# A two-block model on one core: the second block's attention ordered by token tile, its output products between the last groups, and norms kept in PSUM

## The chip, the cores and the metric

The kernel runs on one core of one Trainium2 chip. The time is the device time of one execution in microseconds. One execution was also recorded by the hardware profiler; durations and waits below are from it.

## The reference, cut to what matters

Two blocks of two layers each work on 256 tokens of 1024 features, in float32. The change is in the second block. Each of its layers projects the input, runs three mixers, adds them, normalizes, and runs a feed-forward part:

```
h = x @ w_cols
o_gla  = _gla_mixer(...)      # 4 heads, head norm, times silu(gate)
o_rwkv = _rwkv7_mixer(...)    # 4 heads, head norm, plus bonus, times gate
o_nsa  = _nsa_mixer(...)      # 8 heads: compressed, selected and window attention
mix = jnp.concatenate([o_gla, o_rwkv, o_nsa], axis=-1) @ w_out[l]
x = _layer_norm(DEEPNORM_ALPHA * x + mix, ln1_w[l], ln1_b[l])
ffn = (jax.nn.silu(x @ ffn_w_gate[l]) * (x @ ffn_w_up[l])) @ ffn_w_down[l]
x = _layer_norm(DEEPNORM_ALPHA * x + ffn, ln2_w[l], ln2_b[l])
```

The NSA output is `gt[0] * o_cmp + gt[1] * o_slc + gt[2] * o_win`: the compressed attention (here "block"), the selected one (with 4 blocks of 64 keys and 16 selections it sees every block, so it is causal attention with keys of its own) and the window one.

## The kernel before, in words

Tokens lie in two tiles of 128 partitions. Every engine (PE = TensorE, ACT = ScalarE, DVE = VectorE, POOL = GpSimd, SP = SyncE) runs its own program in the order in which it is written in `second_layers`; semaphores tie them. The same helper names (`nsa`, `gla`, ...) stand in the program of each engine.

Weights are multiplied in two parts of reduced precision. An item is 256 rows by up to 512 columns. SP loads it into one of three raw slots, ACT casts it (`W.high`, L172) into one of four parts slots, POOL subtracts the cast from the raw item (`W.low`, L179), and PE multiplies (`W.multiply`, L210): per item and token tile 2 chunks x 3 products = 6 matmuls of 512 columns. ACT's cast of item k waits until PE has used item k - 4 for both tiles; POOL takes the items in order.

The attention of the selected (kind 0) and window (kind 1) branch comes in 12 groups `GROUPS2`: kind, token tile, key-value group and, in tile 1, a half. `nsa(a)` on PE issues the scores of group a (bank 4), the turn of group a-1's probabilities (bank 5) and the values of group a-2 (bank 0); DVE (`soft`, `output`) reads scores, takes the maximum and scales the sums into `NS`; ACT does the exponentials and copies turned probabilities. Between groups stand the steps of the two recurrent mixers (`gla`, `increment`, `unknowns`, `from_state`, `outputs`). Probabilities live in `sm` and `PT`, which lie in the fourth parts slot, and the block attention's tiles in the third; so no weight of `w_out` is split before the attention is over.

After group 11 come, in this order: the block attention's values (`block_values`, L1471; scores and turn stand before groups 12 and 13 of the pipeline), the turns of `NS` over both tiles, four NSA items of `w_out` (`out_nsa(n)`: columns half n // 2, rows half n % 2, both tiles), the turns of the normed mixer outputs `Y`, and four items for these (`out_mix`), tile after tile. `centre`, `spread` and `scale` on DVE are the head norm; ACT applies its weights into `VAL` (L2022), DVE `mixed` multiplies by gates and splits high and low. `residual` adds `ALPHA * x` in `x` and takes statistics; `layer_norm` normalizes `x` in SBUF in two steps of 1024 columns (L2097). Then `x` is turned and the first gate columns are multiplied tile by tile. The down products use banks 0 and 1.

## Time and profile before

| | us |
| --- | --- |
| median of 3 runs | 1605.82 (1604.97 to 1606.61) |
| the profiled execution | 1605.48 |
| its span | 1603.7 |
| PE busy | 1513.7 |
| POOL busy | 973.1 |
| ACT busy | 788.6 |
| DVE busy | 724.8 |

The span runs from the first to the last recorded instruction. A busy PE is not PE at its peak: matmuls overlap, and the clock granted to it has two levels, 1.2 and 2.4 GHz; the profile gives its mean over a stretch as a share of full speed. An engine's idle time costs something only where another waits for it.

### The profile page before, as it was taken

The page shows a single profiled execution, that of the slowest core. Times are in us where ns is not written, and L with a number is a line of the kernel's source. Part 1 is how long each engine was busy: PE and PEld are TensorE (multiplying, and loading weights), DVE is VectorE, ACT ScalarE, POOL GpSimd, SP SyncE. Part 2 cuts the span into 40 slices and gives each one's busy share as a digit, 9 for nine tenths or more (in the row PEclk, how much of TensorE's full clock was granted, in tenths as well). Part 3 has the DMA queues.
Part 4 walks back from the last instruction along what each step waited for, and adds up shares of the span by engine and source line. Part 5 has one row for each costly group of instructions (what it writes and reads, how often), then busy time and mean ns, then how long its engine had stood idle before and what let it go on. Part 6 is the DMA issues. An engine that isn't in the chain of part 4 may idle for free. (4 is left out here: it accounts for less than half of the span.)

```text
span 1603.7 us, 20620 instructions
## 1 busy us (share of the span) xinstructions
PE 1513.7 (94%) x7896; PEld 1243.0 (78%) x7896; DVE 724.8 (45%) x1078; ACT 788.6 (49%) x1230; POOL 973.1 (61%) x416
## 2 busy tenths in 40 slices
PE   8999999999999998989999889999899998799998
PEld 6887787778886886768788668888688786678886
DVE  3224835562218562625567671110346667721102
ACT  5544575445445664358454434443476443444442
POOL 6887349787884386767200269879774000778785
PEclk9999999999999999999999799999999998899999
DMA  7665335455663255555311136655453310456553
GB/s 228 182 177 165 92 93 179 159 174 166 183 183 106 81 156 182 173 167 148 118 48 54 53 118 201 207 157 205 144 169 96 106 53 1 132 160 188 150 197 131
DMA packets 121632, 227.96 MB, mean 142 GB/s; under 512 B 10304, under 2 KB 26176, under 8 KB 121536
## 3 DMA queue, kind: packets, MB, share of 16 engines
q1 hardware_dynamic: 120384, 222.46, 45.5%
q10 hardware_dynamic: 1152, 4.19, 0.9%
q8 instruction: 63, 1.03, 0.3%
q14 instruction: 33, 0.27, 0.1%
HBM read 225.58 MB, written 1.05 MB: 141 GB/s over the span
## 5 line engine op out<-in xcount | busy, mean ns | idle before, releaser
L179 POOL TENSOR_TENSOR parts<-raw,parts 128x1024 fp32r<-128x1024 f32 (+5 forms) x412 | 972.9, 2376 | 616.4 <-ACT parts L172 614.0
L210 PE MATMUL ps<-parts,xT 128*128 128x512 f32 (+4 forms) x2624 | 819.9, 390 | 20.1 <-issue 4.4
L172 ACT CAST parts<-raw 128x1024 fp32r<-128x1024 f32 (+5 forms) x412 | 415.6, 1013 | 458.6 <-PE ps L210 251.0
L210 PEld LDWEIGHTS ps<-parts,xT 128*128 128x128 f32 x2624 | 493.5, 191 | 128.6 <-issue 10.6
L210 PE MATMUL ps<-parts,x_low 128*128 128x512 f32 (+3 forms) x672 | 254.7, 387 | 0.0
L210 PE MATMUL ps<-parts,M_low 128*128 128x512 f32 (+2 forms) x640 | 245.3, 387 | 0.0
L210 PEld LDWEIGHTS ps<-parts,x_low 128*128 128x128 f32 x672 | 129.1, 192 | 23.7 <-issue 0.5
L210 PEld LDWEIGHTS ps<-parts,M_low 128*128 128x128 f32 x640 | 121.3, 190 | 20.6
L210 PE MATMUL ps<-parts,aT 128*128 128x512 f32 x352 | 109.5, 395 | 0.0
L210 PE MATMUL ps<-parts,H_low 128*128 128x512 f32 x272 | 106.0, 394 | 0.0
L210 PEld LDWEIGHTS ps<-parts,aT 128*128 128x128 f32 x352 | 66.0, 187 | 15.6
L2585 DVE TENSOR_TENSOR EE<-ps,EE 128x512 f32<-128x512 f32 (+1 forms) x24 | 15.3, 646 | 103.5 <-ACT EE L2065 103.3
L706 ACT ACTIVATE H<-ps,st 128x512 f32<-128x512 f32 (+2 forms) x72 | 47.3, 666 | 28.5 <-PE ps L210 28.1
L210 PE MATMUL ps<-parts,ysT 128*128 128x512 f32 x192 | 61.1, 396 | 0.0
L210 PEld LDWEIGHTS ps<-parts,H_low 128*128 128x128 f32 x272 | 51.0, 188 | 12.3
L2592 DVE TENSOR_TENSOR H<-ps,EE 128x512 f32<-128x512 f32 (+1 forms) x24 | 15.5, 647 | 96.4 <-PE ps L210 96.4
L2536 DVE SCALAR_TENSOR_TENSOR x<-x,ps 128x512 f32<-128x512 f32 x16 | 10.9, 679 | 103.7 <-PE ps L210 103.7
L767 ACT ACTIVATE sm<-sm,nmx 128x256 f32<-128x256 f32 (+1 forms) x80 | 36.3, 457 | 29.5 <-DVE nmx L944 29.5
L210 PE MATMUL ps<-parts,mn_high 128*128 128x512 f32 x128 | 44.4, 415 | 0.4 <-DVE mn_low L821 0.4
L1252 PE MATMUL ps<-ident,H 128*128 128x128 f32 x228 | 34.5, 286 | 9.1 <-DVE H L2086 8.0
L1252 PEld LDWEIGHTS ps<-ident,H 128*128 128x128 f32 x228 | 28.6, 147 | 18.2 <-DVE H L2086 12.2
L210 PEld LDWEIGHTS ps<-parts,ysT 128*128 128x128 f32 x192 | 36.1, 188 | 8.5
(340 smaller groups left out, 1825.1 us busy)
## 6 DMA issues: line engine op xcount, KB each, us to landing
raw<-in_w_in SPq DMA_DIRECT2D x160, 512.0 KB, 3.5
raw<-in_ffn_w_down SPq DMA_DIRECT2D x44, 512.0 KB, 4.4
raw<-in_ffn_w_gate SPq DMA_DIRECT2D x40, 512.0 KB, 3.7
raw<-in_ffn_w_up SPq DMA_DIRECT2D x40, 512.0 KB, 3.7
raw<-in_w_out SPq DMA_DIRECT2D x32, 512.0 KB, 3.4
raw<-in_w_branch SPq DMA_DIRECT2D x24, 512.0 KB, 3.3
raw<-in_w_mem_kv SPq DMA_DIRECT2D x16, 512.0 KB, 3.4
raw<-in_w_in SPq DMA_DIRECT2D x16, 366.0 KB, 3.2
```

The source lines that it names most:

```text
L172: self.nc.scalar.copy(self.part(i, 0)[:, 0:nk, 0:w], self.raw(i)[:, 0:nk, 0:w]).then_inc(self.hi_ready.sem, 1)
L179: self.nc.gpsimd.tensor_tensor(self.part(i, 1)[:, 0:nk, 0:w], self.raw(i)[:, 0:nk, 0:w], self.part(i, 0)[:, 0:nk, 0:w], ALU.subtract).then ...
L210: ins = pe.matmul(b[:, 0:w], a(k0 + 2 * n + c, t), self.part(i, lo_w)[:, c, 0:w], start=(opens and n == p == 0), stop=(final and p == len( ...
L706: PJ.empty(lane, nc.scalar.activation(H[:, t, c0:c0 + w], b[:, 0:w], ACT.Sigmoid if s in TAIL_STEPS else ACT.Copy, scale=st[:, 0, t:t + 1] ...
L767: lane.done(nc.scalar.activation(smv(a, j), smv(a, j), ACT.Exp, bias=nmx[:, a, j:j + 1], accum_out=den[:, a, j:j + 1]), p_ok if j == 3 els ...
L1252: ins = pe.transpose(b[:, k * P:(k + 1) * P], src, chip.ident[:])
L2536: banks.empty(lane, v.scalar_tensor_tensor(out=xs, in0=xs, scalar=ALPHA, in1=b[:, :], op0=ALU.mult, op1=ALU.add), ((s, j), t), L)
L2585: PJ.empty(lane, v.tensor_tensor(sg[:, t, 0:w], b[:, 0:w], sg[:, t, 0:w], ALU.mult), (("gt", j), t))
L2592: ins = v.tensor_tensor(H[:, t, c0:c0 + w], b[:, 0:w], sg[:, t, 0:w], ALU.mult)
```

## The change

Seven edits, all in the second block. `GROUPS2` and `SUMS2` run over tiles first, so that all of tile 0's attention is done with group 3. The block attention moves up: its scores before group 6, its turn before 7, its values (into bank 1) before 8 and 9; DVE's and ACT's parts of it move with it. From group 6 on, probabilities go to `KPt` and `BAt`, two tiles of the recurrence that are free by then, and `tmp` to `IC`; so ACT casts the four NSA items between groups 7 and 10, and POOL makes their low parts there. `NS` is turned by tile, and `out_nsa` and `out_mix` take one tile at a time, the first of them before and after the last values. The head norm, the weighting and the mix work in the PSUM banks that the products wrote, ACT takes the squares; `residual` and `layer_norm` work in PSUM in halves of 512 columns and write `x` once, and PE turns each half when it is written. The output columns close half by half: the first half for both tiles, then the second tile by tile. The down products get banks 4 to 7 (`DB`). Of the gate columns' items ACT casts two ahead of the root and two behind the turned `x`, where it cast one and three.

```diff
-GROUPS2 = [(k, t, g, q) for k in range(2) for t in range(NT) for g in range(2) for q in range(t + 1)]
-SUMS2 = [(k, t, g) for k in range(2) for t in range(NT) for g in range(2)]
+GROUPS2 = [(k, t, g, q) for t in range(NT) for k in range(2) for g in range(2) for q in range(t + 1)]
+SUMS2 = [(k, t, g) for t in range(NT) for k in range(2) for g in range(2)]
 G2 = len(GROUPS2)
+BLOCK_AT = 6
+MOVED = 6
...
+    def turn_n(t):
+        pe.wait_ge(*E("ns").at((1, 1 + len(SUMS2) // 4)[t]))
+        turn(("n", t), [NS[:, t, c * P:(c + 1) * P] for c in range(4)])
+    def out_nsa(n, tiles):
+        for t in tiles:
+            TP.taken(pe, ("n", t))
+            if (n, t) == (0, 0):
+                BO.drained(pe, ("block", 1))
+            if (n, t) == (2, 0):
+                pe.wait_ge(*E("o_read").at(len(SUMS2)))
+            W.multiply(pe, ("out_nsa", n // 2), n % 2, by_feature(OT), by_feature(x_lo), [t])
+    def turn_y(t):
+        YB.taken(pe, ("Y", t))
+        turn(("y", t), [Y[:, t, c * P:(c + 1) * P] for c in range(4)])
+    def out_mix(j, n, t):
+        TP.taken(pe, ("y", t))
+        W.multiply(pe, ("out_mix", j), n, by_feature(OT), by_feature(x_lo), [t])
...
     increment(2)
+    block_scores()
     nsa(6)
     from_state(2)
     unknowns(3)
     gla(4)
     from_state(3)
+    block_turn_p()
     nsa(7)
     gla(5)
+    block_values(0)
     nsa(8)
     gla(6)
+    block_values(1)
     nsa(9)
     for par in range(2):
         GB.taken(pe, (("g", LEVELS), par))
     outputs(0)
+    turn_n(0)
     nsa(10)
+    nsa(11)
     outputs(1)
-    nsa(11)
-    block_scores()
     nsa(12)
-    block_turn_p()
+    out_nsa(0, [0])
     nsa(13)
+    out_nsa(1, [0])
+    turn_n(1)
+    out_nsa(2, [0])
+    out_nsa(0, [1])
+    out_nsa(1, [1])
+    turn_y(0)
+    out_nsa(2, [1])
+    out_nsa(3, [0])
+    turn_y(1)
+    out_nsa(3, [1])
+    for n in range(2):
+        for t in range(NT):
+            out_mix(0, n, t)
     for t in range(NT):
-        block_values(t)
-    pe.wait_ge(*E("ns").at(NT))
-    turn(("n", 0), [NS[:, t, c * P:(c + 1) * P] for c in range(2) for t in range(NT)])
-    turn(("n", 1), [NS[:, t, c * P:(c + 1) * P] for c in range(2, 4) for t in range(NT)])
-    for n in range(4):
-        out_nsa(n)
-        if n % 2:
-            t = n // 2
-            pe.wait_ge(*E("normed").at(t + 1))
-            turn(("y", t), [Y[:, t, c * P:(c + 1) * P] for c in range(4)])
-    ST.drained(pe, ("Y", 1))
+        for n in range(2):
+            out_mix(1, n, t)
     for t in range(NT):
-        pe.wait_ge(*E("mixed").at(t + 1))
-        for j in range(2):
-            for n in range(2):
-                W.multiply(pe, ("out_mix", j), n, by_feature(OT), by_feature(x_lo), [t])
-    for t in range(NT):
-        pe.wait_ge(*E("x1").at(t + 1))
         for i in range(2):
+            OB.taken(pe, (("out", i), t))
...
     nsa(6)
+    act.wait_ge(*E("mxc").at(1))
+    lane.done(sc.activation(spare[2][:, 0:256], spare[2][:, 0:256], ACT.Exp), E("pc_exp"))
     between(2)
     decayed(5)
     between(3)
-    for a in range(7, G2 + 1):
-        nsa(a)
-    act.wait_ge(*E("mxc").at(1))
-    lane.done(sc.activation(spare[2][:, 0:256], spare[2][:, 0:256], ACT.Exp), E("pc_exp"))
-    act.wait_ge(*E("pt_full").at(G2 + 1))
-    lane.done(sc.copy(spare[2][:, 256:512], ptb[:, 0:S]), E("pt"))
-    for t in range(NT):
+    act.wait_ge(*E("bpt_full").at(1))
+    lane.done(sc.copy(spare[2][:, 256:512], ptb[:, 0:S]), E("bpt"))
+    def squares(t):
+        act.wait_ge(*E("centred").at(t + 1))
+        lane.done(sc.activation(CUM[:, 2 * t:2 * t + 2, :].rearrange("p m n -> p (m n)"), YB.read(act, ("Y", t)),
+                                ACT.Square), E("squared"))
+    def n_high(t):
+        b = TP.read(act, ("n", t))
+        lane.done(sc.copy(OT[:, 4:8, t * P:(t + 1) * P], b.rearrange("p (c n) -> p c n", c=4)), E("n_high"))
+    def deviation(t):
         act.wait_ge(*E("var").at(t + 1))
         eight = slice(8 * t, 8 * t + 8)
         lane.done(sc.activation(st[:, 2, eight], st[:, 1, eight], ACT.Sqrt), E("sd"))
-    act.wait_ge(*E("o_read").at(len(SUMS2) + NT))
-    W.high(act, W.begin(("out_nsa", 0)) + 1)
-    for i in range(2):
-        b = TP.read(act, ("n", i))
-        lane.done(sc.copy(OT[:, 4 + 2 * i:6 + 2 * i, :], turned(b)), E("n_high"))
-    W.high(act, W.begin(("out_nsa", 0)) + SPLIT - 1)
+    first = W.begin(("out_nsa", 0))
+    nsa(7)
+    W.high(act, first)
+    nsa(8)
+    W.high(act, first + 1)
+    nsa(9)
+    BO.wait_filled(act, ("block", 1))
+    W.high(act, first + 2)
+    n_high(0)
+    nsa(10)
+    W.high(act, first + 3)
+    nsa(11)
+    squares(0)
+    nsa(12)
+    deviation(0)
+    n_high(1)
+    squares(1)
+    deviation(1)
+    W.high(act, first + SPLIT)
+    W.high(act, first + SPLIT + 1)
...
         if k == 0:
-            W.high(act, first_gate)
+            W.high(act, first_gate + 1)
         root(0)
         if k == 0:
+            x1_high(0)
             W.high(act, first_gate + 3)
-            x1_high(0)
         if k == 0 or l == layers - 1:
...
-        b = ST.read(dve, ("Y", t))
+        b = YB.read(dve, ("Y", t))
         TP.taken(dve, ("I", 2 * t + 1))
-        lane.settle()
-        ST.empty(lane, v.tensor_tensor(Y[:, t, :], b[:, :], Y[:, t, :], ALU.add), ("Y", t))
+        tt(b[:, :], b[:, :], Y[:, t, :], ALU.add)
         yv, _, mean, _, _ = norm(t)
         lane.settle()
         lane.done(v.tensor_reduce(mean, yv, AX_X, ALU.add))
         ts(mean, mean, 1.0 / HD, None, ALU.mult)
-        tt(yv, yv, mean.unsqueeze(2).to_broadcast([P, 8, HD]), ALU.subtract)
+        tt(yv, yv, mean.unsqueeze(2).to_broadcast([P, 8, HD]), ALU.subtract, E("centred"))
     def spread(t):
         yv, sv, inv, var, sd = norm(t)
-        tt(sv, yv, yv, ALU.mult)
-        lane.settle()
+        dve.wait_ge(*E("squared").at(t + 1))
...
     def mixed(t):
         n = slice(t * P, (t + 1) * P)
-        TP.taken(dve, ("y", t))
-        tt(VAL[:, 0:2, n], VAL[:, 0:2, n], FT[:, F_GG:F_GG + 2, n], ALU.mult)
-        tt(VAL[:, 2:4, n], VAL[:, 2:4, n], BON[:, :, n], ALU.add, settle=False)
-        tt(VAL[:, 2:4, n], VAL[:, 2:4, n], GT[:, :, n], ALU.mult)
+        b = TP.read(dve, ("y", t)).rearrange("p (c n) -> p c n", c=4)
+        dve.wait_ge(*E("weighted").at(t + 1))
+        tt(b[:, 0:2], b[:, 0:2], FT[:, F_GG:F_GG + 2, n], ALU.mult)
+        tt(b[:, 2:4], b[:, 2:4], BON[:, :, n], ALU.add, settle=False)
+        tt(b[:, 2:4], b[:, 2:4], GT[:, :, n], ALU.mult)
         lane.settle()
-        lane.done(v.tensor_copy(OT[:, 0:4, n], VAL[:, :, n]))
-        tt(x_lo[:, 0:4, n], VAL[:, :, n], OT[:, 0:4, n], ALU.subtract, E("mixed"))
+        lane.done(v.tensor_copy(OT[:, 0:4, n], b))
+        lane.settle()
+        TP.empty(lane, v.tensor_tensor(x_lo[:, 0:4, n], b, OT[:, 0:4, n], ALU.subtract), ("y", t))
+    def n_low(t):
+        b = TP.read(dve, ("n", t))
+        dve.wait_ge(*E("n_high").at(t + 1))
+        n = (slice(None), slice(4, 8), slice(t * P, (t + 1) * P))
+        TP.empty(lane, v.tensor_tensor(x_lo[n], b.rearrange("p (c n) -> p c n", c=4), OT[n], ALU.subtract), ("n", t))
...
     grown(2)
+    block_soft()
     nsa(6)
     step(3)
     gla(4)
+    block_sums()
     nsa(7)
     gla(5)
+    block_output(0)
     nsa(8)
     gla(6)
     nsa(9)
+    block_output(1)
+    nsa(10)
+    n_low(0)
+    nsa(11)
     centre(0)
-    nsa(10)
+    nsa(12)
     spread(0)
-    nsa(11)
-    block_soft()
+    nsa(13)
+    n_low(1)
     centre(1)
-    nsa(12)
+    scale(0)
     spread(1)
-    nsa(13)
-    block_sums()
-    block_output(0)
-    block_output(1)
-    for i in range(2):
-        low(x_lo[:, 4 + 2 * i:6 + 2 * i, :], ("n", i), OT[:, 4 + 2 * i:6 + 2 * i, :], i, "n_high")
-    scale(0)
     scale(1)
     mixed(0)
     mixed(1)
...
     def residual(banks, s, j, t, L=L):
         b = banks.read(dve, ((s, j), t), L)
-        xs = x[:, t, j * HALF:(j + 1) * HALF]
-        banks.empty(lane, v.scalar_tensor_tensor(out=xs, in0=xs, scalar=ALPHA, in1=b[:, :],
-                                                 op0=ALU.mult, op1=ALU.add), ((s, j), t), L)
         lane.settle()
-        lane.done(v.bn_stats(bn[:, t, j, :], xs))
-    def layer_norm(k, t, l=l):
+        lane.done(v.scalar_tensor_tensor(out=b, in0=x[:, t, j * HALF:(j + 1) * HALF], scalar=ALPHA, in1=b,
+                                         op0=ALU.mult, op1=ALU.add))
+        lane.settle()
+        lane.done(v.bn_stats(bn[:, t, j, :], b))
+    def layer_norm(k, t, l=l, L=L):
+        banks, s = ((OB, "out"), (DB, "dn"))[k]
         lane.settle()
         lane.done(v.bn_aggr(mv[:, t, :], bn[:, t, :, :].rearrange("p a b -> p (a b)")))
         ts(mv[:, t, 1:2], mv[:, t, 1:2], LN_EPS, None, ALU.add, e=E("lnv"))
         dve.wait_ge(E("ln_in").sem, 64 * (l + 1))
-        stt(x[:, t, :], x[:, t, :], mv[:, t, 0:1], ln[:, 2 * k, :], ALU.subtract, ALU.mult, settle=False)
+        for j in range(2):
+            b = banks.read(dve, ((s, j), t), L)
+            stt(b, b, mv[:, t, 0:1], ln[:, 2 * k, j * HALF:(j + 1) * HALF], ALU.subtract, ALU.mult, settle=False)
         dve.wait_ge(E("lns").sem, 2 * NT * l + NT * k + t + 1)
         lane.done(v.reciprocal(mv[:, t, 1:2], mv[:, t, 1:2]))
-        stt(x[:, t, :], x[:, t, :], mv[:, t, 1:2], ln[:, 2 * k + 1, :], ALU.mult, ALU.add, E("x2" if k else "x1"))
+        lane.settle()
+        for j in range(2):
+            b, half_ = banks.read(dve, ((s, j), t), L), slice(j * HALF, (j + 1) * HALF)
+            banks.empty(lane, v.scalar_tensor_tensor(out=x[:, t, half_], in0=b, scalar=mv[:, t, 1:2], in1=ln[:, 2 * k + 1, half_],
+                                                  op0=ALU.mult, op1=ALU.add), ((s, j), t), L)
...
+        DB = Banks(ctx, nc, "db", [chip.bank(4 + i) for i in range(4)])
```

What this does to PE's order at the end of the attention, in the first layer (L1430 before and L1444 after are turns of probabilities, L1446 and L1460 values, L1471 block values, L1252 and L1262 turns, L210 products with weights). Before:

```order
L1430 MATMUL ps<-ident,spare_3_7037 128x128 [waits e_pt,e_p]
L1430 MATMUL ps<-ident,spare_3_7037 128x128 x3
L1446 MATMUL ps<-H,spare_3_7037 128x64 [waits e_o_read,e_pt]
L1446 MATMUL ps<-H,spare_3_7037 128x64 x3
L1463 MATMUL ps<-ident,spare_2_7036 128x128 [waits e_pt,e_pc_exp]
L1463 MATMUL ps<-ident,spare_2_7036 128x128
L1446 MATMUL ps<-H,spare_3_7037 128x64 [waits e_pt]
L1446 MATMUL ps<-H,spare_3_7037 128x64 x3
L1471 MATMUL ps<-spare_2_7036 128x512 [waits tp_emptied1,e_pt,e_o_read]
L1471 MATMUL ps<-spare_2_7036 128x512 [waits e_o_read]
L1252 MATMUL ps<-ident,H 128x128 [waits tp_emptied1,e_ns]
L1252 MATMUL ps<-ident,H 128x128 x3
```

After:

```order
L1444 MATMUL ps<-ident,H 128x128 [waits e_pt,e_p]
L1444 MATMUL ps<-ident,H 128x128 x3
L1460 MATMUL ps<-H 128x64 [waits e_o_read,e_pt]
L1460 MATMUL ps<-H 128x64 x3
L210 MATMUL ps<-parts,xT 128x512 [waits w_high_ready,bo_emptied0,tp_emptied1]
L210 MATMUL ps<-parts,x_low 128x512
L210 MATMUL ps<-parts,xT 128x512
L210 MATMUL ps<-parts,x_low 128x512
L210 MATMUL ps<-parts,xT 128x512 [waits w_low_ready]
L210 MATMUL ps<-parts,xT 128x512
L1460 MATMUL ps<-H 128x64 [waits e_pt]
L1460 MATMUL ps<-H 128x64 x3
```

The block values are gone from here, and one tile's product with the first item stands between the values of groups 10 and 11; the wait for `e_ns` has gone to the turn behind it.

ACT's order in the first layer, before from the copy of group 10's turned probabilities on, after from group 9's exponentials on (L1916 and L1950 are such copies, L1909 and L1943 exponentials, L172 casts of weights, L2017 and L2049 high parts of `NS`, L2044 squares, L2012 and L2054 roots). Before:

```order
L1916 COPY spare_3_7037<-ps 128x512 [waits e_o_full,e_pt_full]
L1909 ACTIVATE spare_3_7037,den<-spare_3_7037,nmx 128x256 [waits e_mx]
L1909 ACTIVATE spare_3_7037,den<-spare_3_7037,nmx 128x256
L1916 COPY spare_3_7037<-ps 128x512 [waits e_o_full,e_pt_full]
L2006 ACTIVATE spare_2_7036<-spare_2_7036 128x256 [waits e_mxc]
L2008 COPY spare_2_7036<-ps 128x256 [waits e_pt_full]
L2012 ACT_TABLE_LOAD
L2012 ACTIVATE st<-st 128x8 [waits e_var] x2
L172 CAST parts<-raw 128x1024 [waits w_landed2,w_used,e_o_read]
L172 CAST parts<-raw 128x1024 [waits w_landed0,w_used]
```

After:

```order
L1943 ACTIVATE H,den<-H,nmx 128x256 [waits e_mx]
L1943 ACTIVATE H,den<-H,nmx 128x256
L172 CAST parts<-raw 128x1024 [waits w_landed1,w_used,bo_filled]
L2049 CAST xT<-ps 128x4x128 [waits tp_filled]
L1950 COPY H<-ps 128x512 [waits e_o_full,e_pt_full]
L1943 ACTIVATE H,den<-H,nmx 128x256 [waits e_mx]
L1943 ACTIVATE H,den<-H,nmx 128x256
L172 CAST parts<-raw 128x1024 [waits w_landed2,pj_filled]
L1950 COPY H<-ps 128x512 [waits e_o_full,e_pt_full]
L1943 ACTIVATE H,den<-H,nmx 128x256 [waits e_mx]
L1943 ACTIVATE H,den<-H,nmx 128x256
L2044 ACTIVATE CUM<-ps 128x512 [waits yb_filled,e_centred]
```

Casts, which stood behind everything, stand between the exponentials and the next copy, and the squares ahead of the last copy.

## Rows read from the trace of the kernel before

**Rows 1.** The page: span, and busy time of each engine.

```profile
span 1603.7 us, 20620 instructions
...
PE 1513.7 (94%) x7896; PEld 1243.0 (78%) x7896; DVE 724.8 (45%) x1078; ACT 788.6 (49%) x1230; POOL 973.1 (61%) x416
...
L179 POOL TENSOR_TENSOR parts<-raw,parts 128x1024 fp32r<-128x1024 f32 (+5 forms) x412 | 972.9, 2376 | 616.4 <-ACT parts L172 614.0
```

**Rows 2.** Windows: PE, PEld, DVE, ACT, POOL busy us, granted clock, DMA share, GB/s.

```profile
863.30:959.90 96.60, 80.69 (x446) 65.11 (x447) 71.75 (x117) 41.25 (x85) 34.96 (x14) 0.88 0.21 66
1319.80:1330.30 10.50, 10.50 (x77) 9.87 (x75) 6.60 (x13) 4.61 (x13) 0.00 (x0) 0.84 0.01 2
1330.30:1353.50 23.20, 22.15 (x183) 20.03 (x182) 20.02 (x45) 10.08 (x32) 0.00 (x0) 1.00 0.00 1
1353.50:1366.65 13.15, 6.18 (x14) 2.57 (x13) 8.79 (x22) 5.28 (x8) 3.06 (x2) 0.56 0.00 0
1366.65:1381.40 14.75, 14.74 (x56) 11.63 (x56) 9.05 (x9) 5.48 (x9) 10.67 (x5) 0.82 0.42 143
1381.40:1395.95 14.55, 11.76 (x48) 8.79 (x48) 14.07 (x13) 5.81 (x9) 9.74 (x5) 1.00 0.48 144
1395.95:1401.90 5.95, 2.13 (x10) 1.76 (x10) 5.23 (x6) 1.64 (x2) 5.95 (x2) 0.78 0.63 175
1401.90:1409.45 7.55, 7.55 (x25) 5.91 (x26) 5.45 (x9) 0.79 (x2) 2.53 (x2) 0.72 0.49 140
1409.45:1416.40 6.95, 6.71 (x34) 5.43 (x33) 1.98 (x3) 5.89 (x7) 2.36 (x2) 1.00 0.01 2
1319.80:1416.40 96.60, 81.72 (x440) 65.97 (x439) 71.18 (x115) 39.57 (x80) 34.31 (x14) 0.86 0.22 66
```

**Rows 3.** Waits of PE, 1319.8 to 1416.4: us, times, longest.

```profile
PE ps L1471 <- DVE spare L2086: 4.0, 2, 3.2
PE ps L1252 <- DVE x L2097: 3.8, 1, 3.8
PE ps L210 <- issue: 2.2, 1, 2.2
```

**Rows 4.** Timeline of DVE: start, us, instruction, idle before it.

```profile
1137.43 3.32 DVE L2097 SCALAR_TENSOR_TENSOR x<-x,mv,arena 128x1024 f32<-128x1024 f32 x1
...
1369.15 2.45 DVE L2086 TENSOR_TENSOR H<-H,st 128x512 f32<-128x512 f32 x1
...
1378.21 2.52 DVE L2469 CAST xT<-DL 128x512 fp32r<-128x512 f32 x1
...
1388.60 0.43 DVE L2086 TENSOR_TENSOR DL<-DL,GT 128x256 f32<-128x256 f32 x1
...
1393.35 3.25 DVE L2097 SCALAR_TENSOR_TENSOR x<-x,mv,arena 128x1024 f32<-128x1024 f32 x1
...
1399.79 0.67 DVE L2536 SCALAR_TENSOR_TENSOR x<-x,ps 128x512 f32<-128x512 f32 x1
```

**Rows 5.** Timeline of POOL: four low parts.

```profile
1393.10 11.33 POOL L179 TENSOR_TENSOR parts<-raw,parts 128x1024 fp32r<-128x1024 f32 x4 [4.81 <-ACT parts L172]
```

**Rows 6.** Timeline of ACT: two casts of weights, and the norm's weighting.

```profile
1362.46 1.99 ACT L172 CAST parts<-raw 128x1024 fp32r<-128x1024 f32 x2 [6.24 <-DVE spare L2086]
...
1375.41 1.51 ACT L2022 ACTIVATE DL<-ps,vec2s 128x128 f32<-128x128 f32 x4 [4.83 <-PE ps L1252]
```

**Rows 7.** Timeline of PE: a wait at the layer change, one at 1319, block products.

```profile
1140.80 1.09 PE L1252 MATMUL ps<-ident,x 128*128 128x128 f32 x8 [2.53 <-DVE x L2097]
...
1319.12 0.71 PE L1574 MATMUL ps<-H 64*128 64x128 f32 x4 [1.30 <-DVE H L2483]
...
1348.35 1.92 PE L1455 MATMUL ps<-spare,arena 128*128 128x32 f32 x16
...
1356.78 2.07 PE L1471 MATMUL ps<-spare 128*128 128x512 f32 x2 [3.21 <-DVE spare L2086]
```

**Rows 8.** The chain that ended last: start, us, what.

```profile
1463.55 22.18 PE ps L210 x96
```

122 lines of the change are left out of this document (67 added, 55 removed).

## The prediction

> **What bounds the kernel now.** I read the page first: TensorE (PE) is busy for 1513.7 of 1603.7 us [rows 1], so only some 90 us of idle time, and time at the lower clock, can be won. Then the windows: in the first of the second block's two layers, 863.3 to 959.9, PE is busy for 80.69 us of 96.60, in the second, 1319.8 to 1416.4, for 81.72 [rows 2]. The two are one picture 456.5 us apart, so I work out one and count it twice. The stretch runs from the third state increment to the end of the first gate columns; the change touches no other place but the layer change and the very end.
>
> The windows by stage show where that stretch loses. From 1353.5 to 1366.65 PE works 6.18 us of 13.15 at a mean granted clock of 0.56: block values, sums and turns of the attention output, one after another. From 1381.4 to 1401.9 it idles twice more (2.79 and 3.82 us) [rows 2]. Its waits say for whom: DVE's block sums (4.0), the layer norm's `x` (3.8), the mix (2.2, shown as issue) [rows 3]. Why DVE is late stands in its timeline: with POOL at work a 128x512 product of two SBUF operands took 2.45, a cast 2.52, a 128x1024 step of the layer norm 3.25, while `x<-x,ps`, with one operand in PSUM, took 0.67 in the same stretch of POOL work, 1393.10 to 1404.43 [rows 4, 5].
>
> Ledger of the 96.6 us: idle 96.60 - 81.72 = 14.9. A clock of 0.84, 0.56, 0.82, 0.78 and 0.72 means that a share of twice the missing part was granted 1.2 instead of 2.4 GHz (32, 88, 36, 44, 56%); half of the busy time in that share is lost: 1.7 + 2.7 + 2.7 + 0.5 + 2.1 = 9.7. Left is work at full clock: 81.7 - 9.7 = 72.0.
>
> **The change, part by part.** No product of PE is added or removed, so the 72.0 stay. What changes are the waits and the clock. I walk PE's new order from 1319.8 with the durations of before. One tile of one output piece is 6 matmuls of 22.18/96 = 0.231 us [rows 8], so 1.4.
>
> *Groups by token tile.* The first tile's four sums are done before the stretch; one of them adds a multiply and an add on DVE ahead of a step PE waits for: +0.4.
>
> *Block attention moved up.* `block_scores` (1.92 [rows 7]) stands before group 6, and group 6's scores now wait for DVE to read its bank: idle 0.6, before these two reads came behind the scores at no cost. Two block values (2.07 each at the low clock [rows 7], 1.06 at the upper) go between groups, where their inputs are long ready: the 4.0 and the wait for the turns behind them go. Late next is DVE, 20.02 of 23.2 us busy there [rows 2]; the moved sums and outputs (some 4.5 us of DVE) stand against one sum taken out ahead of it and 6 us of PE work put between the groups.
>
> *Weights split during the attention.* Four casts of 1.0 [rows 6] enter ACT between groups 7 and 10, behind the exponentials, ahead of the copy of the next group's turned probabilities, which PE needs later: nothing. But each releases a POOL instruction of 2.4 [rows 1], and the attention has DVE steps with two SBUF operands. Bounds for a lock: 0 and 2.5 (the 128x512 product [rows 4]). Walked through, `block_output(0)`, the sum of groups 4-5, `block_output(1)` and `output(6)` wait 0.7, 1.9, 0.8 and 0.8; PE has other work behind most of it: idle 0.5 before the turn of group 10. The 1.9 falls on a 128x4 product, a size that no row shows under POOL.
>
> The Trainium skill (SBUF — State Buffer, "Who interferes with whom") says that a DVE instruction with two SBUF inputs and a GpSimd one that reads SBUF exclude each other for the whole instruction, whoever issues first. The trace agrees at 2.45 against 0.67. It speaks against this part, and for the PSUM part; taken for every size it gives the walk above, and with small steps exempt some 2 us less a layer.
>
> *Output products between the last groups.* `values(11)` stands behind ACT's `squares(0)`, and that behind `centre(0)` on DVE, 4 steps of up to 0.7: idle 1.1. Then turn, high part and low part of tile 1 hide behind the 1.4 of the pieces around them; `turn_y(0)` waits 0.3 for `scale(0)`.
>
> *Norm and mix.* All eight NSA pieces end near 1370.7, against 1381.4 before. The mix is late next: DVE's `spread(1)`, the root, then on ACT two casts (2.0), only then the weighting (1.51) [rows 6], then `mixed(0)` on DVE in PSUM, 3 x 0.43 + 2 x 0.7 = 2.9 with gaps, against 2.52 + 2.7 for its last two steps before: ready at 1373.3, idle 2.6. `mixed(1)` ends 2.9 later and one piece (1.4) lies between: idle 1.5.
>
> *Output columns half by half.* The last two pieces of tile 0 end 2.8 before the last product. The norm then takes 1.5 (sum, statistics), 0.5 (aggregate), 1.3 (first pair, halves of 0.67), 0.1, 0.75 (first half of the last pair): idle 4.2 - 2.8 = 1.4 for the first turn, instead of 3.82. POOL can't hold it, since all steps read PSUM. Then 0.8 until the first product (0.5 for the high part, 0.3 at the second tile).
>
> *Casts of the gate columns.* Only two of the four are ahead of the root now; two stand behind `x1_high(0)`. Their low parts need 1.0 + 2.4 and another 2.4: PE waits 1.3 and 1.0 in the first tile.
>
> Idle after: 0.4 + 0.6 + 0.5 + 1.1 + 0.3 + 2.6 + 1.5 + 1.4 + 0.8 + 1.3 + 1.0 = 11.5. Before, the clock fell after idle of 3.8 us, after 7.0 in pieces, and also around one wait of 1.30 at 1319 [rows 2, 7]. I keep the 1.7 of the first window and one drop as priced at 1401.9 (2.1) [rows 2]: 3.8; bounds 0 and 9.7. Layer: 72.0 + 11.5 + 3.8 = 87.3 against 96.6, gain 9.3, twice 18.6.
>
> *Layer change.* PE waits 2.53 for `x` there [rows 7], whose last step took 3.32 under POOL [rows 4]. As two halves in PSUM of 0.67 it ends 2.0 sooner, and the first turn needs only the first of them. I take 2.2 for both tiles; bounds 1.3 (something else is as late) and 3.2 (all 2.5, and a half step at the second tile). *The end*: four steps of 512 take what two of 1024 did; 0.
>
> Sum: 18.6 + 2.2 = 20.8 off the profiled execution's 1605.48 (its span of 1603.7 and 1.8 around it), 0.3 under the median of 1605.82: 1584.7, I say 1585.
>
> **Rivals.**
> *A. The clock holds and small steps pass POOL.* PE's gaps become many and short instead of few and long, and 23.2 us with 1.05 idle ran at 1.00 [rows 2]. Without the 3.8 and the 2 of locks per layer: 1584.7 - 11.6 = 1573. Against it: the drop around 1.30 us of idle at 1319 [rows 7].
> *B. Each of the four locks falls on the path in full.* DVE is 86% busy in the attention, and sets PE's scores. 4 x 2.5 = 10 on PE's path, of which the walk's 0.5, 1.1 and some of the mix's wait hold about 3: +7 a layer, 1599. Against it: the PE work now lying between the groups.
> *C. POOL bounds the gate columns.* The first tile consumes a piece in 1.4, POOL makes one in 2.4 to 2.8 [rows 1, 5]. If all four came late: 4 x 2.6 - 5.6 = 4.8 instead of 2.3, 1590. Against it: two are split during the mix.
> *D. Slower: the lower clock takes the attention.* If the locks thin PE's work between groups so far that 1.2 GHz is granted there, matmul time doubles, and each us of full-clock work costs another. It decides from 10.4 us of such work a layer beyond what the forecast holds (20.8/2); with 14 the time is 1584.7 + 28 = 1613. Before, a stretch of 11.6 us at the low clock went with 7.0 us of idle [rows 2], and the attention's 23.2 us with 1.05 of idle had none.
> *E. It doesn't overlap:* a wait in ACT's order (the split behind the block values) holds the turned copies back, and PE's tail only moves. Then the loss of 1353.5 to 1381.4 (7.0 idle, 5.4 clock) stays instead of 3.9 (0.5, 1.1, 0.3 and half of the clock's 3.8): a layer gains 9.3 - 8.5 = 0.8, in all 3.8, 1602.
>
> **Chances.** Forecast 0.50, A 0.19, B 0.14, C 0.08, D 0.05, E 0.04. About 3.2 us (0.2%) is what a measurement tells from no change. Faster 0.92, same 0.03, slower 0.05. Likeliest case's own range 1578 to 1592; eight times in ten 1571 to 1599.
>
> **What would show it.** The window from 1353.5 on has no stretch at 0.56, and PE's idle over the same work is 10 to 12 us, not 14.9. DVE steps with two SBUF operands between groups 7 and 11 take up to 2.5 where POOL works, the norm's halves 0.67 always. PE waits for `mixed(0)` 2 to 3 us, for the norm's first half 1 to 2, for POOL in the gate columns about 2. I am wrong if PE waits over 3 us anywhere in the attention (B or D), if the clock there is under 0.9, or if the mix is ready before the NSA pieces end (A and more).

## The result, and the profile after

The changed kernel takes 1599.35 us (median of 20 runs, 1592.0 to 1620.29) where the kernel before takes 1608.15 in the same rounds: a ratio of 0.995, 95% interval 0.9935 to 0.9966, so 8 to 9 us faster. Run once more, unaltered, on another chip it was 1592.05 beside 1605.73, ratio 0.9909 (0.9891 to 0.9928): 14 us. The forecast was 1585, 20.8 us off. The direction was right; the size was too large by 12 to 13 us on the first chip and by 7 on the second.

The two kernels differ in how much one execution differs from the next. The kernel before keeps within 1600 and 1615 on all chips; the changed one goes from 1587 to 1620, and its time follows its mean granted clock: 1592.0 at 0.983, 1599 near 0.979, 1608.3 at 0.970, 1620.3 at 0.962, 1.1 us for each 0.001 in a line through the 20. All ratios here leave out executions more than 1.5% above the fastest of their kernel, which the medians keep; the profile that came with the result is of such an execution (1620.3), so the readings below are from the repeat (1594.34 us, clock 0.981).

The page of that execution, its span and the first section, against [rows 1]:

```profile
span 1593.0 us, 20692 instructions
...
PE 1518.0 (95%) x7896; PEld 1247.3 (78%) x7896; DVE 701.7 (44%) x1090; ACT 788.7 (50%) x1234; POOL 964.8 (61%) x416
```

DVE's work is 23 us less than before; TensorE's is 4 us more, although no product was added. Where that comes from stands in four windows (busy time of each engine, then the granted clock): from the first state increment to the end of the third, and from there to the turn of x1's second tile, in both layers. First of before, then of after.

```profile
852.95:864.75 11.80, 10.15 (x86) 9.05 (x87) 7.43 (x17) 6.32 (x19) 0.00 (x0) 1.00 0.60 178
864.75:952.25 87.50, 72.58 (x407) 58.42 (x406) 69.21 (x112) 33.57 (x73) 31.96 (x12) 0.86 0.23 73
1308.00:1319.85 11.85, 10.19 (x86) 9.10 (x87) 7.43 (x17) 6.21 (x19) 0.00 (x0) 1.00 0.63 178
1319.85:1409.40 89.55, 74.91 (x406) 60.45 (x406) 69.20 (x112) 33.68 (x73) 31.95 (x12) 0.85 0.23 71
```

```profile
852.05:867.90 15.85, 15.10 (x85) 13.84 (x85) 9.58 (x22) 6.32 (x19) 0.00 (x0) 0.68 0.45 133
867.90:948.25 80.35, 70.14 (x398) 55.71 (x399) 57.24 (x109) 32.65 (x67) 28.43 (x12) 0.96 0.24 73
1301.35:1318.20 16.85, 16.61 (x84) 14.86 (x84) 9.10 (x21) 6.06 (x19) 0.00 (x0) 0.59 0.45 126
1318.20:1398.65 80.45, 70.30 (x399) 55.80 (x399) 57.12 (x109) 32.64 (x67) 28.41 (x12) 0.96 0.24 73
```

The forecast's stretch is, but for gate columns at its end, the second and the fourth row: 87.50 to 80.35 and 89.55 to 80.45, 16.3 us gained where 18.6 were forecast. The second layer gained 9.1 of the 9.3 forecast, the first only 7.2: it was 2 us shorter before, so working out one layer and counting it twice took too much. The lower clock there went from 0.86 and 0.85 to 0.96. But the rows above them, the state chain, went from 11.80 to 15.85 and from 11.85 to 16.85: the same products at a granted clock of 0.68 and 0.59 instead of 1.00. TensorE's busy time there rose by 4.95 and 6.42, its idle time fell by 0.90 and 1.42. Of those 9.1 us the forecast has only its 0.4 a layer for the added sum. With 2.7 at the layer change, 0.9 gained ahead of the first increment and nothing at the end, that is 16.3 + 2.7 + 0.9 - 9.1 = 10.8, but for rounding the difference of the spans (1603.7 - 1593.0 = 10.7). Over the whole span TensorE's idle time fell by 15.0 us (90.0 to 75.0) where the forecast had 9.0, and its busy time rose by 4.3 where the forecast had it fall by 11.8.

What TensorE waited for in the forecast's stretch, in place of [rows 3] (us in total, times, longest):

```profile
PE ps L210 <- DVE x_low L2530: 3.1, 2, 2.0
PE ps L210 <- POOL parts L179: 1.8, 2, 1.1
PE ps L1262 <- DVE x L2622: 1.5, 1, 1.5
PE ps L1460 <- ACT H L1950: 1.1, 1, 1.1
PE ps L1444 <- ACT H L1943: 0.7, 1, 0.7
PE ps L1430 <- DVE spare L2154: 0.6, 1, 0.6
PE ps L1262 <- DVE H L2516: 0.6, 1, 0.6
PE ps L1430 <- DVE H L2154: 0.6, 1, 0.6
```

With two of 0.2 that are left out, together 10.4; the forecast had 11.1 here, and 0.4 ahead of it. The waits of 4.0, 3.8 and 2.2 us are gone.

### The profile page after: what moved, and what is told of

Read it like the earlier page. It is cut to its first block and busy times, and to the rows that moved or that the text cites. A ratio compares the mean times of both kernels' runs of the same rounds, so it can differ in the third digit from the quotient of the medians.

```text
span 1619.0 us, 20692 instructions
## 1 busy us (share of the span) xinstructions
PE 1544.4 (95%) x7896; PEld 1268.1 (78%) x7896; DVE 705.7 (44%) x1090; ACT 787.7 (49%) x1234; POOL 965.2 (60%) x416
## 5 line engine op out<-in xcount | busy, mean ns | idle before, releaser
L210 PE MATMUL ps<-parts,xT 128*128 128x512 f32 (+4 forms) x2624 | 818.2, 389 | 21.9 <-DVE x_low L2530 5.7
L172 ACT CAST parts<-raw 128x1024 fp32r<-128x1024 f32 (+5 forms) x412 | 415.5, 1012 | 439.5 <-PE ps L210 240.5
L210 PEld LDWEIGHTS ps<-parts,xT 128*128 128x128 f32 x2624 | 491.1, 190 | 130.3 <-ACT parts L172 10.8
L210 PE MATMUL ps<-parts,x_low 128*128 128x512 f32 (+3 forms) x672 | 253.9, 386 | 0.0
L210 PE MATMUL ps<-parts,M_low 128*128 128x512 f32 (+2 forms) x640 | 244.5, 386 | 0.0
L210 PEld LDWEIGHTS ps<-parts,x_low 128*128 128x128 f32 x672 | 128.5, 191 | 23.0 <-issue 0.5
L210 PEld LDWEIGHTS ps<-parts,M_low 128*128 128x128 f32 x640 | 120.7, 189 | 20.4
L210 PE MATMUL ps<-parts,aT 128*128 128x512 f32 x352 | 110.1, 395 | 1.2 <-POOL parts L179 1.2
L210 PE MATMUL ps<-parts,H_low 128*128 128x512 f32 x272 | 106.0, 394 | 0.0
L210 PEld LDWEIGHTS ps<-parts,aT 128*128 128x128 f32 x352 | 66.0, 188 | 17.6 <-POOL parts L179 2.1
L2602 DVE SCALAR_TENSOR_TENSOR ps<-x,ps 128x512 f32<-128x512 f32 x16 | 11.1, 696 | 116.8 <-PE ps L210 115.8
L210 PE MATMUL ps<-parts,ysT 128*128 128x512 f32 x192 | 61.1, 396 | 0.0
L210 PEld LDWEIGHTS ps<-parts,H_low 128*128 128x128 f32 x272 | 51.0, 188 | 12.2
L210 PE MATMUL ps<-parts,mn_high 128*128 128x512 f32 x128 | 44.0, 412 | 0.9 <-DVE mn_low L821 0.4
L210 PEld LDWEIGHTS ps<-parts,ysT 128*128 128x128 f32 x192 | 36.1, 188 | 8.5
L1262 PE MATMUL ps<-ident,H 128*128 128x128 f32 x228 | 33.8, 280 | 7.3 <-DVE H L2143 4.9
L1262 PEld LDWEIGHTS ps<-ident,H 128*128 128x128 f32 x228 | 27.5, 144 | 14.7 <-DVE H L2143 6.8
```

The source lines that it names most:

```text
L172: self.nc.scalar.copy(self.part(i, 0)[:, 0:nk, 0:w], self.raw(i)[:, 0:nk, 0:w]).then_inc(self.hi_ready.sem, 1)
L210: ins = pe.matmul(b[:, 0:w], a(k0 + 2 * n + c, t), self.part(i, lo_w)[:, c, 0:w], start=(opens and n == p == 0), stop=(final and p == len( ...
L1262: ins = pe.transpose(b[:, k * P:(k + 1) * P], src, chip.ident[:])
L2602: lane.done(v.scalar_tensor_tensor(out=b, in0=x[:, t, j * HALF:(j + 1) * HALF], scalar=ALPHA, in1=b, op0=ALU.mult, op1=ALU.add))
```

## The experiments

Each time stands beside the kernel before on the same chip in the same rounds. The kernels before of different rows ran on different chips, so rows are compared by their ratios. In the table "clock" is the range of the mean granted clock over a kernel's executions. Each name says what the kernel starts from, "before" or "changed".

| kernel | us, median | before | ratio, 95% interval | clock |
|---|---|---|---|---|
| changed, again | 1592.05 | 1605.73 | 0.9909 (0.9891 to 0.9928) | 0.981-0.987 |
| before + group order | 1609.22 | 1605.73 | 1.0023 (1.0012 to 1.0034) | 0.969-0.973 |
| before + group order, sum late | 1605.55 | 1605.95 | 1.0003 (0.9988 to 1.0018) | 0.970-0.981 |
| before + 16 products of 32 columns | 1614.30 | 1606.23 | 1.0052 (1.0035 to 1.0069) | 0.971-0.973 |
| before + norm in PSUM | 1604.47 | 1605.73 | 0.9990 (0.9980 to 1.0001) | 0.972-0.981 |
| the same + order of gate casts | 1598.09 | 1605.60 | 0.9950 (0.9936 to 0.9964) | 0.975-0.981 |
| changed + transposes in chain | 1597.37 | 1605.73 | 0.9940 (0.9920 to 0.9960) | 0.976-0.989 |
| changed, sum late | 1594.11 | 1605.95 | 0.9931 (0.9907 to 0.9956) | 0.978-0.987 |
| changed, sums mixed | 1598.67 | 1605.95 | 0.9940 (0.9915 to 0.9965) | 0.961-0.985 |
| the same, casts late | 1595.14 | 1605.95 | 0.9931 (0.9917 to 0.9946) | 0.980-0.985 |
| changed, sum late, states early | 1621.52 | 1605.60 | 1.0079 (1.0055 to 1.0103) | 0.945-0.981 |
| the same, squares late | 1632.97 | 1605.60 | 1.0168 (1.0116 to 1.0219) | 0.945-0.962 |
| the same, fifth level moved | 1622.78 | 1605.60 | 1.0084 (1.0052 to 1.0116) | 0.959-0.975 |
| changed, sum late, dense fill in chain | 1590.75 | 1606.23 | 0.9902 (0.9880 to 0.9924) | 0.984-0.995 |
| changed, sum late, transposes in chain | 1599.65 | 1606.23 | 0.9948 (0.9925 to 0.9971) | 0.977-0.989 |
| the dense fill, attention too | 1586.30 | 1606.23 | 0.9882 (0.9860 to 0.9904) | 0.986-0.994 |
| the same, mix and norm too | 1587.40 | 1605.12 | 0.9879 (0.9854 to 0.9903) | 0.990-0.995 |
| before + dense fill | 1595.22 | 1605.12 | 0.9938 (0.9918 to 0.9959) | 0.989-0.994 |

### 1. The changed kernel again

No edit. 

> The changed kernel once more, unaltered. Theory of the clock: the walk of waits was about right (in the first layer of the profiled execution 84.6 us stand where 96.6 stood), and the 14 us that the median of 1599 lacks to 1585 are time at 1.2 GHz, which starts at the two waits of 0.8 and 0.7 us in the state chain (850 and 852 us) and in some executions lasts through the attention. Then the times spread over more than 10 us with the mean granted clock, by some 1.3 us for each 0.001 of it, and the drop near 852 and 1302 is there again, of another length. Rival, a fixed cost (locks, the new order of the groups): the times keep within 5 us of their median and the clock explains no more than 2 us.

The low clock near 856 and 1303 us was there again; the spread on this chip was small (five executions, 1586.9 to 1594.3; a sixth, of 2969.64 us at a clock of 1.0, is unexplained and left out of the ratio; without it the median is 1590.98). This is how the low clock begins. TensorE around the first increment, then DVE in the same time (start, duration, instruction, in brackets the idle time before it and its releaser):

```profile
852.06 1.13 PE L1599 MATMUL ps<-H 64*128 64x128 f32 x8 [0.76 <-ACT LD L2012]
853.92 0.37 PE L1605 MATMUL ps<-H 64*128 64x128 f32 x1 [0.73 <-DVE H L2545]
```

```profile
849.90 0.17 DVE L2314 RECIPROCAL fac<-den 128x4 f32<-128x4 f32 x1
850.53 0.17 DVE L2143 TENSOR_TENSOR fac<-fac,gate 128x4 f32<-128x4 f32 x1 [0.46 <-DVE fac L2314]
850.73 0.42 DVE L2143 TENSOR_TENSOR IC<-ps,fac 128x256 f32<-128x256 f32 x1
851.19 0.42 DVE L2143 TENSOR_TENSOR H<-H,IC 128x256 f32<-128x256 f32 x1
...
853.59 0.28 DVE L2545 COPY H<-EE 64x256 f32<-64x256 f32 x1
```

Four steps of the third group's sum, `fac` to `H<-H,IC`, 1.7 us with their wait, stand ahead of the state step `H<-EE` at 853.59, for which the increment waits 0.73. There is the forecast's "one of them adds a multiply and an add on DVE ahead of a step PE waits for: +0.4", at 1.8 times its price in this layer and about half of it (0.23) in the other. What follows it is larger, in windows of 5 us (the granted clock is the first of the last three numbers):

```profile
850.00:855.00 5.00, 3.50 (x27) 3.09 (x26) 3.36 (x9) 2.34 (x7) 0.00 (x0) 1.00 0.52 154
855.00:860.00 5.00, 5.00 (x25) 4.44 (x24) 3.51 (x9) 2.85 (x9) 0.00 (x0) 0.58 0.92 265
860.00:865.00 5.00, 5.00 (x30) 4.78 (x30) 2.76 (x7) 0.46 (x1) 0.00 (x0) 0.50 0.01 4
```

### 2. The group order, and one sum

```diff
-GROUPS2 = [(k, t, g, q) for k in range(2) for t in range(NT) for g ...
-SUMS2 = [(k, t, g) for k in range(2) for t in range(NT) for g ...
+GROUPS2 = [(k, t, g, q) for t in range(NT) for k in range(2) for g ...
+SUMS2 = [(k, t, g) for t in range(NT) for k in range(2) for g ...
```

On the kernel before, alone: 

> The kernel before with the groups ordered by token tile, nothing else. Theory that the order brings the drop in the state chain: the clock falls at about 1300 to 1310 us and near 855, and stays low for 10 us or more, time 2 to 8 us over the kernel before. Theory that the order is innocent: the 0.4 us a layer of the forecast, between 0 and +1.5 us in all, and the clock in 840 to 870 us at 0.95 or more.

3.5 us slower, with low stretches behind the first increment in both layers. In the profiled execution the three increments take 5 to 6 us more in each layer; in the second, the kernel before has a low stretch behind the third increment (0.83 from 1320 to 1330), which this one lacks (0.58 there while the chain still runs, then 1.00), so part of it comes back. Then the same with the sum behind the step:

```diff
-                nsa(4)
+                nsa(4, summed=False)
...
                 grown(0)
+                output(2)
                 nsa(5)
```

> The kernel before with the groups ordered by token tile and the third group's sum moved behind the first state step. The order alone gave 1609.2 beside 1605.7. Theory of the sum: back to the kernel before, within 1.5 us of it, and no low stretch of 13.7 us at 854 and 1315. Rival: still 3 us above it.

Back to the kernel before (1.0003). The windows 850 to 870, order alone and then with the sum late, and of the latter one window in the second layer:

```profile
850.00:860.00 10.00, 8.51 (x44) 7.32 (x42) 5.58 (x15) 4.41 (x15) 0.00 (x0) 0.69 0.73 210
860.00:870.00 10.00, 10.00 (x59) 9.07 (x59) 5.85 (x14) 3.10 (x9) 0.00 (x0) 0.62 0.01 3
```

```profile
850.00:860.00 10.00, 8.77 (x69) 7.89 (x69) 7.77 (x17) 4.11 (x11) 0.00 (x0) 1.00 0.52 129
860.00:870.00 10.00, 7.83 (x70) 6.84 (x69) 7.38 (x18) 5.29 (x15) 0.00 (x0) 1.00 0.23 84
...
1310.00:1320.00 10.00, 8.90 (x49) 7.75 (x50) 6.15 (x16) 4.57 (x15) 0.00 (x0) 0.69 0.70 211
```

So in the kernel before one sum ahead of the state step costs some 3 us (the two intervals overlap by a little, 1.0012 to 1.0018), and by the windows of the first layer it is clock. The second layer says that the sum isn't the only way in: in this execution (1610.51 us, one of the slower of its twelve) the increment waits for no sum, and the clock still falls at 1314, behind one wait of 0.87 us, for 10 us. In the changed kernel moving the sum should have brought 6 to 12 us:

> The changed kernel with one sum of the groups moved on DVE: the one of the third group runs behind the first state step instead of ahead of it. Theory that the sum opens the door to the low clock: ahead of the step it costs 1.9 us of DVE, the first increment waits 0.7 us (0.3 in the second layer) behind a wait of 0.8, and the clock falls for 10 to 14 us. With the sum behind the step the second wait goes, the clock stays up in 840 to 870 us and 1300 to 1320, first to third increment take 8.7 to 10 us instead of 14 to 15, and the time is 1580 to 1586 where the changed kernel had 1592. Rival, the clock falls there in any case because of what the groups of the first tile hold: time within 3 us of the changed kernel.

It did not (0.9931, not to be told from 0.9909). The first low stretch went, and TensorE then waited 1.08 us twice, in the second and third increment; the clock fell behind the second of these, where the changed kernel has its block scores:

```profile
863.11 0.71 PE L1605 MATMUL ps<-H 64*128 64x128 f32 x4 [1.08 <-DVE H L2549]
863.75 1.97 PE L1469 MATMUL ps<-spare,arena 128*128 128x32 f32 x16
866.30 2.07 PE L1430 MATMUL ps<-arena 64*128 64x256 f32 x4 [0.58 <-DVE spare L2154]
```

The last of these rows takes 2.07 us, where the same products take 1.13 at full clock.

Nor did another order of the sums help, which keeps the fifth group free of one (`SUMS2 = [(0,0,0), (0,0,1), (0,1,0), (1,0,0), (1,0,1), (0,1,1), (1,1,0), (1,1,1)]`):

> The changed kernel with another order of the sums: the first group of the second tile before the second kind of the first, so that no sum falls into the group ahead of the first state step (as in the kernel before). Theory of the sum: as for the kernel with the sum moved, 1578 to 1586. The first tile's sums are ready one group later, which turn_n(0) may wait for: up to 0.5 us a layer. Rival as there: 1590 or more, with a low stretch of over 10 us behind the first increment.

1598.67, from 1589 to 1622; a low stretch behind the third increment in both layers of the profile.

### 3. The block scores' place

```diff
                 increment(2)
+                pe.wait_ge(*E("sc_read").at(6))
+                pe.wait_ge(*E("kblk").at(1))
+                for t in range(NT):
+                    for c in range(4):
+                        pe.matmul(scb[...], qT[:, c, t * P:(t + 1) * P], kblk, start=True, stop=True)
                 nsa(6)
```

> The kernel before with the 16 products of 32 columns that the changed kernel has behind the third increment, here without a reader (1.1 us of TensorE at full clock). If this light work behind the third wait is what lets the clock fall there, a low stretch of 7 us or more between 861 and 880 and 4 to 10 us slower than the kernel before. If it is only work: 0 to 2.2 us slower and the clock up there.

8.1 us slower. The 8 calls are recorded as 16 products, and they are not the 1.1 us that was expected: [rows 7] has them at 1.92 us, in a window at full clock [rows 2]. So 3.5 to 3.8 of the 8.1 us are their own time in two layers, and some 4.4 come on top. The kernel before and then this one, 860 to 870:

```profile
860.00:870.00 10.00, 8.70 (x74) 8.01 (x72) 6.92 (x15) 5.19 (x16) 0.00 (x0) 1.00 0.06 23
```

```profile
860.00:870.00 10.00, 8.70 (x44) 8.10 (x44) 4.26 (x8) 2.85 (x7) 0.00 (x0) 0.65 0.01 2
```

In this layer the clock stays up behind a wait of 1.3 us in the one and falls behind the same wait in the other. In the second layer it falls in both, for 3 to 4 us in the kernel before (0.83 from 1320 to 1330) and for some 10 in this one. In the repeat of the changed kernel the clock had fallen before the block scores began; with the sum moved they stand where it falls. So they are a second way in, and would explain why undoing the first did not help. The changed kernel with its block scores moved back was not run.

### 4. Filling the waits

First with transposes of the identity, before the first increment (6), in each increment (3) and before group 6 (4):

> The changed kernel with 6, 3 a step and 4 transposes without a reader put into TensorE's waits of the state chain (before the first increment, before the unknowns of each increment, before group 6). Theory of the clock: with the waits filled the low stretches at 850 and 1302 us go, the attention runs at 2.4 GHz in nearly every execution, mean clock 0.985 or more, median 1580 to 1592, spread half of the changed kernel's. Rival, the fill is only work on the path: some 19 transposes of 0.13 us a layer, half of them hidden, 2 to 3 us slower than the changed kernel, with the same clock.

No gain on the changed kernel (0.9940 against 0.9909): the chain's second and third increment still waited (1.5 us), and the low stretch came 8 and 11 us later. Then with work that is there anyway: on top of the late sum, `from_state(1)` and `from_state(2)` each moved ahead of the increment that waits:

```diff
                 unknowns(1)
+                from_state(1)
                 increment(1)
                 gla(3)
-                from_state(1)
                 unknowns(2)
+                from_state(2)
                 increment(2)
                 block_scores()
                 nsa(6)
-                from_state(2)
```

> The changed kernel with the third group's sum behind the first state step, and the products from the state of the second and third chunk ahead of the increments instead of behind them: 1.3 us of work that was there anyway now lies in the two waits of 1.1 us in the state chain. Theory of the clock (a wait there, with little else around it, opens a low stretch of 7 to 14 us, and filling it with work that is there anyway closes it): no low stretch in 840 to 885 and 1290 to 1335 us, 2.2 us of idle a layer gone too, time 1582 to 1589. Rival, the low stretch only moves to the next wait, as it did with the transposes and with the sum moved: within 3 us of those kernels, 1591 to 1597.

1621.52, 16 us slower than the kernel before, where 1582 to 1589 was expected, the largest miss of the study. The waits of 1.08 went; in their place stands one of 2.34, for ACT's copy out of the bank that the moved product fills. Its row, and then the clock behind it:

```profile
862.95 1.22 PE L1614 MATMUL ps<-SP,DL 128*128 128x128 f32 x4 [2.34 <-ACT H L2027]
```

```profile
870.00:890.00 20.00, 19.42 (x83) 16.71 (x84) 10.48 (x25) 6.44 (x16) 1.19 (x1) 0.50 0.00 0
890.00:910.00 20.00, 20.00 (x71) 14.75 (x70) 11.25 (x17) 5.02 (x12) 5.33 (x3) 0.50 0.15 53
910.00:930.00 20.00, 20.00 (x84) 17.88 (x84) 8.80 (x17) 6.82 (x15) 2.87 (x2) 0.50 0.15 53
930.00:940.00 10.00, 9.36 (x42) 6.91 (x42) 5.08 (x12) 1.71 (x4) 0.00 (x0) 0.94 0.00 0
```

From 890 on TensorE is busy for 20.00 of 20 us, and it is granted 1.2 GHz through the whole attention; the full clock comes back at 931, where the NSA output columns of 512 begin. That is what rival D described, though no lock set it off. The wait of 2.34 stands right ahead of it; no run takes that wait alone out, so that it is the cause is not shown. Two edits on top of it, ACT's `squares(0)` behind `nsa(12)`, and the fifth level's products ahead of group 6, were meant to take out the next waits:

> The kernel with the states early, and in it ACT's squares of the first tile behind the last group's copy instead of ahead of it. The wait of 1.1 us of values(11), which the forecast named, goes: 2.2 us off in two layers if nothing else is as late, and the low stretch that begins at 899 or 1347 us in some executions begins less often: 2 to 8 us faster than the states early. Rival: the copy then waits for something else on TensorE or DVE, within 1 us.

> The same, and the fifth level's products between the block scores and group 6, where TensorE waits 0.6 us for the block's softmax to read the bank. Another 1.2 us in two layers, 0 to 3 us faster than the squares late, by the theory of the clock; nothing, if DVE sets the pace of the chain.

1632.97 and 1622.78, where 2 to 8 us less than the states early, and up to 3 less again, were expected: no gain shows at this clock. Most executions of the states early and the squares late come in groups, near 1621 and near 1645; their profiles, one from each group, show the attention at 1.2 GHz in one layer, and in both.

Then both kinds of work at the same places, the sum late in both: before the first increment 3, in the second and third 4, before group 6 2 products (5, 7 and 4 transposes).

```diff
+                def filler(n, copies):
+                    pe.wait_ge(*E("pt").at(copies))
+                    for _ in range(n):
+                        pe.matmul(ptb[:, :], xT[:, 0, 0:P], xT[:, 0:2, :].rearrange("p c s -> p (c s)"), start=True, stop=True)
```

> The changed kernel with the third group's sum behind the first state step, and products of 128x512 without a reader put into the waits of the state chain: 3 before the first increment, 4 in each of the next two, 2 between block scores and group 6 (0.23 us each). Theory that light work around a wait starts the low stretch and dense work keeps the clock: no low stretch in 840 to 885 and 1290 to 1335, 1582 to 1590. Rival, the wait alone counts and these fills hide in it: the same result for the transposes. Rival, the low stretch comes a few us later all the same: 1592 to 1598.

> The same with transposes of 128x128 in place of the dense products, as long in all (5, 7 and 4 for 3, 4 and 2). If the kind of work counts, low stretches of 7 to 14 us behind the chain as in the kernels before, some of them long, 1592 to 1605. If only the waits count, as fast as the dense fill.

0.9902 against 0.9948, on one chip; the intervals just miss each other. Against its own base, the late sum alone (0.9931), the dense fill in the chain is not clear of noise. The profiled execution with dense products has no low stretch from the chain to the gate columns, in either layer; the other keeps the clock in the chain and loses it in the attention (dense first):

```profile
850.00:870.00 20.00, 19.50 (x146) 16.24 (x145) 13.35 (x32) 8.01 (x24) 0.00 (x0) 1.00 0.27 103
...
890.00:910.00 20.00, 17.01 (x106) 13.75 (x106) 15.13 (x29) 7.78 (x17) 2.36 (x1) 1.00 0.16 54
910.00:930.00 20.00, 16.30 (x71) 12.31 (x69) 12.25 (x25) 9.17 (x16) 14.27 (x6) 1.00 0.52 148
```

```profile
850.00:870.00 20.00, 18.84 (x150) 16.43 (x148) 14.23 (x34) 8.18 (x22) 0.00 (x0) 1.00 0.33 107
...
890.00:910.00 20.00, 18.72 (x105) 17.00 (x105) 13.37 (x21) 8.84 (x20) 5.71 (x3) 0.74 0.25 80
910.00:930.00 20.00, 16.25 (x67) 11.89 (x66) 11.74 (x25) 8.13 (x16) 9.43 (x4) 0.89 0.28 80
```

So in the chain both fills held the clock, in the first layer of these two executions. They are no fair pair: the dense one is the fastest of its six (1583.21), the other the slowest of its seven (1602.02). That the dense kind is better rests on the ratios, not on a place. Filling the attention's waits as well (2 and 3 around group 11's scores, 4 before the last values), and then those of mix and norm (6, 4, 5):

> d_chain, and dense products in the attention's three waits as well: 2 before group 11, 3 between its scores and the turn, 4 before the last group's values, 2.1 us in waits of 2.3. By the theory of the clock the low stretches of 1347 and 899 us go too, mean clock 0.985 or more in every execution, 1578 to 1586, spread under 6 us. Rival, the fills come on top: 2 to 4 us slower than d_chain.

> d_all, and dense products in the waits of the tail: 6 and 4 before the first mix products (waits of 1.9 and 1.2 us), 5 before the turn of x1 (1.5 us). If low stretches still begin there in some executions, 1 to 4 us faster than d_all's 1586, mean clock 0.993 or more. If not, the same time within 1.5 us.

1586.30 and 1587.40, ratios 0.9882 and 0.9879: the fastest versions here, for 22 and 37 products a layer that nobody reads. The first is clear of the changed kernel's result (0.995), and of the late sum alone (0.9931, on the same chip); from the repeat's 0.9909 it can't be told. The tail's fill adds nothing. Nor do the fills always hold the clock: in the profiled execution of the first (1593.87, the slowest of its six) it fell at 1317 in the second layer, behind the block scores, with dense products in each wait of the chain (0.90 and 0.76 in the two windows from 1310 to 1330), and again from 1370 on. The control is the kernel before with fills in its own waits, 45 a layer:

> The kernel before with dense products of 128x512 without a reader in its own waits: 3 and 5 in the state chain, 19 at the block attention and its sums (waits of 4.0 and 1.5 us), 6 before the mix, 12 before the norm. Its ledger had 9.7 us of clock loss a layer in the stretch. If the fills take back most of that, and each hides in its wait: 12 to 18 us faster than before, 1588 to 1594, and the change itself is worth only the idle it removes, 3 to 8 us beside d_all. Rival, the clock that falls in a wait costs nothing while TensorE waits, and the fills delay: 1600 or more. The change at a held clock is then worth 15 us or more.

1595.22, 9.9 us off with no other edit, its mean clock up from 0.976 to 0.990. Where both kernels have fills and keep a mean clock of 0.99, the change is thus worth 0.9882 / 0.9938 = 0.9944, 9 us, with the two intervals between 4 and 14 (the two ratios are of different chips). On one chip, against the version with the tail filled too, the medians 1595.22 and 1587.40 are 7.8 us apart.

### 5. The norm in PSUM, and the casts

Residual sums and layer norm of the changed kernel in the kernel before, nothing else: 

> The kernel before with the residual sums and the layer norm kept in PSUM (and the down products in banks of their own), all else as before. The forecast's terms: 2.2 us at the layer change, and in each layer two steps of 3.25 us that become pairs of 1.35, of which the first turn needs one and a half: 2 to 4 us of the wait of 3.8 a layer go. In all 5 to 9 us faster, 1597 to 1601 beside 1605.8. Rival: DVE is late there with the mix of the second tile, not the norm; then only the layer change is won, 2 us.

Only 1.3 us, not to be told from none. The rival was right that something else is late, but it is not the mix: ACT's fourth gate cast waits for its columns to land, and stands ahead of the copy that TensorE then waits 3.33 us for (ACT, then TensorE):

```profile
941.24 1.04 ACT L172 CAST parts<-raw 128x1024 fp32r<-128x1024 f32 x1 [3.25 <-DMA raw<-in_ffn_w_gate]
942.19 1.06 ACT L2042 CAST xT<-ps 128x512 fp32r<-128x512 f32 x2
```

```profile
942.82 1.65 PE L210 MATMUL ps<-parts,xT 128*128 128x512 f32 x3 [3.33 <-ACT xT L2042]
```

```diff
-                        W.high(act, first_gate)
+                        W.high(act, first_gate + 1)
                     root(0)
                     if k == 0:
-                        W.high(act, first_gate + 3)
                         x1_high(0)
+                        W.high(act, first_gate + 3)
```

> The kernel before with the norm in PSUM, and the casts of the gate columns in the changed kernel's order: two ahead of the root, two behind the copy of x1's high part. The norm alone gave 1.3 us, since ACT's cast that waits for a transfer stood ahead of that copy and TensorE waited 3.3 and 3.8 us for it. Theory that this cast is what ate the norm's gain: 4 to 7 us faster than the norm alone, 1597 to 1601. Rival, POOL's low parts are then late instead: within 2 us of the norm alone.

1598.09, 0.995 against 0.999: 6.4 us for this move once the norm is fast. The norm in PSUM alone brought nothing that can be measured; what the order of the casts brings without it was not run.

### 6. POOL beside the attention

On the mixed order, ACT's four casts behind groups 10 and 11 instead of 7 to 10: 

> The changed kernel with the mixed order of sums, and the four casts of the NSA output columns behind groups 10 and 11 instead of 7 to 10, so that POOL does not work while DVE does the attention's steps with two SBUF operands. Forecast's bookkeeping: the locks (some 4 us of DVE) go, of which 0.5 us a layer and part of the 1.1 behind group 11 lie on the path; the parts of the first columns come 2.4 us apart and the last 7 us later, 0 to 3 us of waiting for POOL. Between 1 us a layer faster and 2 us a layer slower than the mixed order. Rival B of the forecast (each lock falls on the path in full): 7 us a layer faster.

0.9931 beside 0.9940. The waits of 0.55 and 0.72 us that the locks caused went, and one of 3.16 took their place: the last cast waits 2.66 us for its columns to land, and the copy for `values(11)` stands behind it. So this run doesn't price the locks by themselves; rival B (7 us a layer) is out by those two waits, 1.3 us a layer.

## Why the prediction came out as it did

*The step that failed* is the last of the ledger: "I keep the 1.7 of the first window and one drop as priced at 1401.9 (2.1) [rows 2]: 3.8", with the sentence it rests on, "the change touches no other place but the layer change and the very end". The clock was booked inside one stretch. In the profiled repeat the stretch kept its clock nearly as forecast (0.96), and the state chain ahead of it, which had 1.00 before, lost 9.1 us. The forecast's own text had both edits that let the clock fall there, the added sum and the block scores, each priced in waits (0.4 and 0.6 us) and not in what the clock does behind them. Put into the kernel before by themselves they cost 3.5 us, and 4.4 us beyond the products' own time. In the repeat it is behind the sum that the clock falls; the block scores take its place when the sum is moved. What makes the clock fall in one execution and not in the next stays open, since it also fell where neither was at work (section 2, second layer). So the term that failed is the clock's: forecast 11.8 us less busy time, measured 4.3 more. On the first chip half of the executions had a mean clock of 0.978 or less, and the one trace from it has its longest low stretch in the second layer's attention (below); that the other 5 to 7 us of the miss lie there is read from this one trace and from the line of time against clock, and no run singles it out.

*Groups by token tile*: 0.73 and 0.23 us for the 0.4. *Block scores*: 0.58 for 0.6. *The output products between the last groups*: 1.1 for values(11) as forecast, 0.6 for turn_y(0) against 0.3, 0.72 for the turn of group 10 against 0.5, and 0.55 for its neighbour's scores that was not in the list. *Norm and mix*: 2.0 and 1.2 us for 2.6 and 1.5. *Norm's first half*: 1.45 for 1.4. *POOL's gate parts*: 1.8 for 2.3. *The first product behind the turn*: 0.24 for 0.8. *Layer change*: 2.7 for 2.2. *The end*: 0. Smaller, but a miss too: one layer was worked out and counted twice, and the first had 2 us less to give.

*The locks* came as walked, the small ones too. DVE beside POOL, then POOL (the 128x4 product, then the block outputs' sums, then a step with an operand in PSUM):

```profile
884.19 0.16 DVE L2143 TENSOR_TENSOR fac<-fac,gate 128x4 f32<-128x4 f32 x1
...
887.98 1.08 DVE L2143 TENSOR_TENSOR H<-H,IC 128x512 f32<-128x512 f32 x1
...
893.72 1.41 DVE L2143 TENSOR_TENSOR fac<-fac,gate 128x4 f32<-128x4 f32 x1
...
895.69 0.69 DVE L2385 TENSOR_TENSOR IC<-ps,facc 128x512 f32<-128x512 f32 x1
896.41 2.17 DVE L2143 TENSOR_TENSOR H<-H,IC 128x512 f32<-128x512 f32 x1
```

```profile
892.75 2.36 POOL L179 TENSOR_TENSOR parts<-raw,parts 128x1024 fp32r<-128x1024 f32 x1 [4.24 <-ACT parts L172]
895.67 2.36 POOL L179 TENSOR_TENSOR parts<-raw,parts 128x1024 fp32r<-128x1024 f32 x1 [0.56 <-ACT parts L172]
```

A product of 128x4 took 1.41 us where it takes 0.16 without POOL, a sum of 128x512 took 2.17 (the one at 887.98 met only the end of a POOL instruction that ran from 886.14 to 888.51), and `IC<-ps,facc`, with PSUM in it, 0.69 beside the same POOL instruction. By the rule that the forecast drew from the Trainium skill (SBUF — State Buffer, "Who interferes with whom"), size would not matter; the trace agrees.

*The rivals.* A (the clock holds) was seen only with fills, and not in each execution; the small steps do not pass POOL. B and C are out: locks cost 1.3 us a layer of waiting, POOL 1.8. E is out: the copy behind the block values waits 0.24. D was given 0.05 and a price of 28 us. What it describes, the attention at 1.2 GHz, is real, while its reason, locks that thin the work, is not shown. The three kernels with the states early were 16 to 27 us over the kernel before, and in the changed kernel's 1620 us execution the granted clock was 0.64 over the second layer's attention:

```profile
1320.00:1420.00 100.00, 95.12 (x374) 76.42 (x375) 54.26 (x105) 32.50 (x67) 27.20 (x12) 0.64 0.17 53
```

Without its clock terms the forecast has 3.4 a layer and 2.2, 9.0 us; with fills in both kernels 9 were measured, between 4 and 14, which fits but is no sharp test. What failed is the 11.8 us of clock.

## What to carry to other kernels

When the lower clock is a term of the sum, book it over the whole kernel, and look first at the stretch just ahead of an edit in which TensorE has short waits and short products: that it ran at 1.00 before says little, since a wait of 0.7 us added there cost 3.5 us, and 1.9 us a layer of narrow products cost 8, over twice their own time. Put products of 128x512 without a reader into a kernel's waits, and into those of the version it is compared with: they took 10 us off the one and 6 to 13 off the other (the 6 within the noise), and show how much of the difference may be clock. And where ACT casts weights, ask of each cast which transfer it waits for and what stands behind it: twice here one such cast ate what another edit had won.

## What the hardware showed that was not expected

- A granted clock of 1.2 GHz does not have to end when TensorE is busy. It lasted from 870 to 930 us with 59.4 of 60 us busy, and ended as the output products began. Why one execution of a kernel falls for 7 us and the next for 60 is open. The Trainium skill (TensorE: Matmul & The Clock Gate, Part 1: The HAM clock gate) says that the throttled level is the default and activity releases it; these rows, busy and at the lower level, don't bear it out as it stands.
- The loss need not stand where the edit is. With the states early, TensorE had one wait of 2.34 us in the chain, and the kernel was 16 us over the kernel before; the low clock stood behind the wait, through the attention.
- Between two chips the same pair of kernels gave ratios of 0.995 and 0.9909, intervals apart. Each was measured in one set of rounds, so whether it is the chip that makes the difference is not shown.
- A DVE step of 128x4 is not free beside POOL: 1.41 us for 0.16.
